# Another order of steps on four engines, in all four phases of a hybrid block kernel

## The reference

```
def first_block(x, meta_tokens, ...):
    h = jnp.concatenate([meta, x], axis=1)                # 272 tokens
    p = rms_norm(h, norm_mix_pre[l]) @ w_in[l]
    oa = rg_lru_group(xa, ya, ...)                        # causal conv, gates, associative scan, gelu
    ob = forgetting_attention_group(q, k, v, f_logit, ..) # 8 heads of 64
    oc, v_own = rwkv7_group(pc, ...)                      # 4 heads of 64, state S per step
    mixed = jnp.concatenate([oa, ob, oc], axis=-1) @ w_out[l]
    h = h + rms_norm(mixed, norm_mix_post[l])
    f = causal_dwconv(rms_norm(h, norm_ffn_pre[l]) @ ffn_up[l], ffn_conv[l])   # 1024 -> 5632
    gate, val = jnp.split(f, 2, axis=-1)
    h = h + rms_norm((gelu(gate) * val) @ ffn_down[l], norm_ffn_post[l])
    return h[:, N_META:]

def second_block(x, ...):
    for l in range(2):
        proj = rmsnorm(x, pre_g[l]) @ w_in[l]
        y_a = sgu_mixer(...) * silu(z_a)                  # layernorm, 128x128 mixing per group
        y_b = mla_mixer(...) * silu(z_b)                  # low-rank attention with rope
        y_c = chunk_band_mixer(...) * silu(z_c)           # banded attention with relative bias
        br = einsum(ys, w_branch[l]);  gates = sigmoid(g_logits + gate_b[l])
        x = x + rmsnorm(sum(gates * br) @ w_out[l], post_g[l])
```

## Time and profile before

| | us |
|---|---|
| median of 3 runs | 941.23 |
| lowest, highest | 940.35, 943.87 |
| span of the profiled execution | 940.6 |
| PE busy | 918.4 (98%) |
| PE weight loads busy | 855.0 (91%) |
| DVE busy | 696.6 (74%) |
| ACT busy | 521.6 (55%) |
| POOL busy | 226.8 (24%) |
| DMA | 150.32 MB, mean 160 GB/s |

### The profile page before, as it was taken

The page is one execution under the profiler, slowest core; times in us unless marked ns, Lnnn a source line. Parts: engine busy times, 40 slices in busy tenths (PEclk is TensorE's granted clock), DMA queues, the critical chain, the costliest instruction groups (busy, mean ns, idle before and its releaser), DMA issues.

```text
span 940.6 us, 19615 instructions
## 1 busy us (share of the span) xinstructions
PE 918.4 (98%) x7924; PEld 855.0 (91%) x7924; DVE 696.6 (74%) x1072; ACT 521.6 (55%) x942; POOL 226.8 (24%) x194
## 2 busy tenths in 40 slices
...
GB/s 320 180 157 113 70 26 2 68 113 180 183 189 185 184 178 180 170 176 245 179 140 153 152 136 203 192 188 181 100 305 152 146 125 177 183 178 181 159 201 45
DMA packets 41705, 150.32 MB, mean 160 GB/s; under 512 B 4624, under 2 KB 5008, under 8 KB 41360
## 3 DMA queue, kind: packets, MB, share of 16 engines
...
## 4 chain that ended last, share of the span: by engine, by line
PE 89%; DVE 4%; ACT 2%; issue 2%; DMA 1%; POOL 1%; DVEq 0%; SPq 0%; ACTq 0%; POOLq 0%
PE ps L736 87%; PE ps L1073 2%; DVE wlo L1713 1%; DMA raw<-in_ws 1%; DVE S L1713 1%; ACT whi L1297 1%; PE ps L1189 0%; DMA h<-in_hT 0%; ACT xh L1297 0%; DVE xl L1721 0%; POOL ocf L2306 0%; ACT L1297 0%; ACT tmp L1297 0%; DVE ht L1721 0%; DVE pcraw L1713 0%
## 5 line engine op out<-in xcount | busy, mean ns | idle before, releaser
L1297 ACT ACTIVATE whi<-raw 128x1024 fp32r<-128x1024 f32 (+1 forms) x265 | 278.2, 1052 | 282.1 <-PE ps L736 276.5
L736 PE MATMUL ps<-xh,whi 128*128 128x256 f32 (+2 forms) x1440 | 412.9, 287 | 4.5 <-ACT xh L1297 1.8
L736 PE MATMUL ps<-xl,whi 128*128 128x256 f32 (+2 forms) x1440 | 407.9, 283 | 2.3 <-DVE xl L1721 2.2
L736 PE MATMUL ps<-xh,wlo 128*128 128x256 f32 (+2 forms) x1440 | 407.0, 283 | 0.0
L1713 DVE TENSOR_TENSOR wlo<-raw,whi 128x1024 fp32r<-128x1024 f32 (+1 forms) x257 | 328.0, 1281 | 103.8 <-ACT whi L1297 103.1
L736 PEld LDWEIGHTS ps<-xh,whi 128*128 128x128 f32 x1440 | 271.5, 189 | 10.9 <-issue 8.3
L736 PEld LDWEIGHTS ps<-xl,whi 128*128 128x128 f32 x1440 | 270.9, 188 | 3.9 <-DVE xl L1721 3.5
L736 PEld LDWEIGHTS ps<-xh,wlo 128*128 128x128 f32 x1440 | 272.0, 189 | 0.0
L736 PE MATMUL ps<-yh,whi 128*128 128x256 f32 x232 | 65.3, 282 | 0.0
L736 PE MATMUL ps<-yl,whi 128*128 128x256 f32 x232 | 65.2, 281 | 0.0
L736 PE MATMUL ps<-yh,wlo 128*128 128x256 f32 x232 | 65.2, 281 | 0.0
...
## 6 DMA issues: line engine op xcount, KB each, us to landing
raw<-in_ws SPq DMA_DIRECT2D x261, 512.0 KB, 3.4
...
```

The costliest lines, as they stand in the source:

```text
L736: return e.matmul(o, l, r, start=start, stop=stop, skip_group_check=True)
L1297: return e.activation(o, a, f, bias=bias, scale=scale, accum_out=acc)
```

## The change

Only the letter strings of `WEAVE` change, those of PE, DVE, ACT and POOL in each of the four phases; SP's strings stay. In each phase every letter stands as often as before in an engine's string, so each engine does the same steps and the same instructions, and within a line in the same order; what changes is how the lines are woven. The semaphore waits follow from the events as before.

- Start: on ACT `la.a` moves from ahead of `inend` to behind split 16; parts of entering tiles stand ahead of splits, and on POOL the first square sums.
- Mixer: on PE the dense tiles of A stand ahead of later doubling steps; `beat` 0 to 4 leave the scan and the output steps and stand in a row ahead of the first `op`, `beat` 5 and 6 stand behind `opend`. On DVE, splits 25 and 26 move from around `lr.tan` 0 to behind attention tile 5; `lr.b` and the LRU scan go to a later place. On ACT, `rw.o` 1 goes ahead of a copy of attention tile 4.
- First seam: on DVE split 35 moves from behind residual 0 to behind all eight entering tiles, on ACT as well.
- Feed-forward and layers: on DVE, ACT and POOL, splits stand in runs of three to six instead of by turns with the evacuations; POOL takes no weight part from unit 35 on, so its "w" letters there issue nothing.

The diff, cut to the mixer, and DVE's string of the feed-forward (the others and the layers' are changed in the same manner):

```diff
 WEAVE = {
     "mixer": {
         "pe": (
-            "ddddddddddfdddddddddrddddddrrdddddddrrrddddfdddddddrrddeddrrrsssdrdrdlrdrdldrddrssrseeessseosoorre"
-            "eerrrrrrozrororeroozrerereeozozrorrroeozerrzorzrroppppppppp"
+            "ddddddddddfddddddrddddddddrrddddrrrfddddddddrrddddddddrrreddddsssdeddddrlrrlerreddrsssrsssoersrero"
+            "orrrrrorroreoooreerereerooroorrreererroorrozzzzzpppppppppzz"
+        ),
+        "dve": (
+            "dwdwdmdwdddwdsdddddwwmmwdwmfmddmwwwdrdrwdmdrfwwwrrrrrdrddwwwmfrdddwwrrwmrrdssrrrewddwwssnssddelder"
+            "rlrwewdrrllrsessslssoorrdorererrrrrreoorrrooerlooollrreeereoowwosreerrroorrccccpppwwwwwpppwwpwpp"
         ),
         "act": (
-            "eodwdwdddwwddwdsdndwwwwfwwrwsrwwrwrrrrwrrwwwrrwwdddddwwrrwwserewlrwlwlrdwdresslseesocorrrererooooo"
-            "eeceoooeeroerroerrrrroocccpwwpwppwpwpwpwpp"
-        ),
-        "dve": (
-            "dmwdwdddwwwdddsdnddwddfwwwdmdfdwwmwsrrddmdmmdwwrdwmmwwmddwdrrwrrrrdwwdrsssdfwrrrwerwrrrwddssrdreee"
-            "edlrwdlrrwldwwldrrssssslssoolllrroererrrerrororooreroooerrcerereooreoeroorrrrcccpwwpwwpppwpwpwpp"
+            "dwedwddwddwdddwsdwwwwrrrwwworfwwwrrrrrrwwwnswwrrrddddwwwwwwsdeerlrllrdersswwweesoosrldrrerooooeeee"
+            "ooooeecrrcoreorrrrerroocccppwwppwwwwpppwpp"
         ),
         "pool": (
-            "wwewwedmoopdddddddwdwwwmmwwwwmmwwwwrrmrmmwwwwrrrwwwwsswrrrwwreeeweerrwwwwllcoooooeeeeeoooooceeeooo"
-            "rrcpppwwwwpppp"
+            "dwwdddmdddddwwowwwmmwwmrewwrwwmmmwmrwwwwrrrwwwwwwwseerrrrrsrwoooeeeeeeooopooowwwolwwleeeeeeooooccr"
+            "recpppwppwpwwp"
         ),
...
     "ffn": {
...
+        "dve": (
+            "hhhdhhdddhhhddddwwwddddcdwwwwccwddcvvcdddccvdwwwwdccwddwwvccvcwddwwcccddvcwdddvwwwwvcccdddcdwwwvvc"
+            "ccwwwddvcccvddwwwddvcccdddwwwwwvccccddddvvwwwcccdddwwvvwwwwwwccwwcdddvwwwwwcccdccwwwwwvvvwwww000w0"
+            "00w101101110w000011111110w1ww"
         ),
...
-        "dve": (
-            "hwdhhhhdhddhhddwddwwdddwddwcdwcdwvcwdcdwvcwdcwdvcdwcwdvcwdcwdvwcdwcdwvcdwcwdvcwdcwdvcwdcwdvwcdwcdw"
-            "vcwdcwdvcwdcdvwcwdcwvdcwdcwdvwcdwcdwvcwdcdwvcdwcvwdcdwcdvwcwdcvwdcdwcwdvcwcvwccvwwwwwwwwwwwww0000w"
-            "0011w0101110w1101000011111www"
-        ),
```

More of the change, by code:

```diff
@@ L264 @@
         "pe": (
[L265 to L266 removed]
+            "ddddddddddfddddddrddddddddrrddddrrrfddddddddrrddddddddrrreddddsssdeddddrlrrlerreddrsssrsssoersrero"
[4 more added lines that the diff above has]
+            "rlrwewdrrllrsessslssoorrdorererrrrrreoorrrooerlooollrreeereoowwosreerrroorrccccpppwwwwwpppwwpwpp"
         ),
         "act": (
[L269 to L274 removed]
+            "dwedwddwddwdddwsdwwwwrrrwwworfwwwrrrrrrwwwnswwrrrddddwwwwwwsdeerlrllrdersswwweesoosrldrrerooooeeee"
+            "ooooeecrrcoreorrrrerroocccppwwppwwwwpppwpp"
         ),
         "pool": (
[L277 to L278 removed]
+            "dwwdddmdddddwwowwwwmmwwmrewwrwwmmmwmrwwwwrrrwwwwwwwseerrrrrsrwoooeeeeeooopooowwwolwwleeeeeeooooccr"
+            "recpppwppwpwwp"
         ),
@@ L285 @@
         "pe": (
-            "ddqdddddddddddddddddddddddddddddddddddddddddddddqdddqqdppppppppppppppppppppppppppppppppppppppppppp"
-            "p00pp1100p11pppppr"
+            "ddqddddddddddddqdddddddddddddddddqddddddddddddddddqddddppppppppppppppppppppppppppppppppppppppppppp"
+            "p00pp1001ppp11pppr"
+        ),
+        "dve": (
+            "hhhdhhdddhhhddddwwwddddcdwwwwccwddcvvcdddccvdwwwwdccwddwwvccvcwddwwcccddvcwdddvwwwwvcccdddcdwwwvvc"
+            "ccwwwddvcccvddwwwddvcccdddwwwwwvccccddddvvwwwcccdddwwvvwwwwwwccwwcdddvwwwwwcccdccwwwwwvvvwwww000w0"
+            "00w101101110w000011111110w1ww"
         ),
         "act": (
-            "wddddqddwddwbwdwccwccwvwccwvvwccwvvwcwvvccwwvcvwcwvcwvcwcwvvwcwvvcwcwvcvwcwvcwvcwcwvvwcwvvcwccvwvw"
-            "cwvcvwcwcvwvcwcwvvwqccwvvwcvwqvqccwcvwvwcvwcvcwwvcvwvwvwvbwwwwwwwwwww00w00w01w00111111000001111w1w"
+            "ddddddddwwwwdccccwwwwvvvcccvvwwwcvvbccwcwwwwvvvcwvwwccccvvqcwqwwwwvvcccvvccwwvvvcwwwcwqvvvcccwwvvv"
+            "cccwwwwwvvvccccwvvvvccwwwqccwwwvvwwccwvwwwvvwwwwwwvccccwwwwvvvvvwwwwb000w0w01w001111100001110w111w"
             "wrrr"
         ),
-        "dve": (
-            "hwdhhhhdhddhhddwddwwdddwddwcdwcdwvcwdcdwvcwdcwdvcdwcwdvcwdcwdvwcdwcdwvcdwcwdvcwdcwdvcwdcwdvwcdwcdw"
-            "vcwdcwdvcwdcdvwcwdcwvdcwdcwdvwcdwcdwvcwdcdwvcdwcvwdcdwcdvwcwdcvwdcdwcwdvcwcvwccvwwwwwwwwwwwww0000w"
-            "0011w0101110w1101000011111www"
-        ),
         "pool": (
-            "dwwwwwwwwwwwwhwwwwwwwwwwwwwwwwwwwwwwwwwwwwwwwwwwwwwwwwwwwwwwwwwwwwwwwwwwhhhhhhhdddddddvvvvvvvvvvvv"
-            "vvvvvvvvvv"
+            "hwwwwwwwwwwhwwwwddwwwwwwwwhhwwhhddddddwwwwvwwwwwvwvvvwwwwwwwwwwwvvwwwwvvvwwwvvwwhwwwwwvvvvvwvvwwww"
+            "wwwhvvvwww"
         ),
@@ L308 @@
         "pe": (
-            "dddddtdtdddddeoododddddddddeeeddeoddoddeooeeoddedeedodooeoeedeeeeddddddddddddoodooeoodedddodossddd"
-            "dddddddddddddddddddddddddddddddddddddddddpppppppppppppppp00p11p0011ppprppp"
+            "dddddtdtdddddeoddddddddddeedddddedeooodoooeeeddddedeeoodedooooeeddeeddddeeddddoeoooedddddooddddsso"
+            "dddddddddddddddddddddddddddddddddddddddddpppppppppppppppp00p11p0011ppppppr"
+        ),
+        "dve": (
+            "wwddddwwdwdwttddwwwwdddeeeddwwwddddddowwooddwwwwwyyoeeoeeddddeyyoowddwwwoeeeeeewwoddddoooyyyyyywww"
+            "eeeuuyywwwweoouuwwooossssssosswwweeddddwwwwoodddwwddwwwddddwwwddsswwwdddddwwwwwdddwwddddddwdddwwdd"
+            "ddwwwdddddwwwmddmmmmdddddwwwwmmmwwww000w0001w111011001110w00001111w1ww"
         ),
         "act": (
[L313 to L320, removed]
+            "wwwwawwtttwowwwwweeeddwdddddwwddwooewwddwwoeeeddwwwwooodeeeewweoeooeddddddswwwweooodeewwwwwoeessso"
+            "oosssswwwwddddowowwwwwwoewwwwsswwwwwdddddddddddddddwwwwwwwwbmdddwwddmmmwwwwmmwwwmmwwwwwb00w000w111"
+            "001111w000001111w1wrrrw"
         ),
         "pool": (
-            "oeoeyyyyyyyywwwwwwwwwwwwwwwwwwwwwwwwwwwwwwwwwwwwwwwwwwwwwwwwwwwwwwwwwwwwwwwwwwwwwwwwwwwwwwwwwwwsss"
-            "saaaateedoodeooeoeeeoeeeeeooooooyeeeeeyyyoooooesssssossmmmmmmmm"
+            "wwwwwwwysssayatwwwywawwwwwawwwswwwwwwweeeooowdweeeewwwyyydeywwwwwowwwwwwwwwoooooeeyyywwwwwwwwwwwww"
+            "wwwwwwwwywwwwwwooowweeeywwwwwwwwwooooooeeeeeessssseoossmmmmmmmm"
         ),
```

20 lines of the change are left out of this document (9 added, 11 removed).

## The result

The changed kernel takes 951.5 us (median of 4 runs, 949.75 to 952.21) against 941.24 for the one before: ratio 1.0102, 95% interval 1.0087 to 1.0117. Forecast were 933 and a range of 928 to 943. The profiled execution's span is 950.3 us, 9.7 over the 940.6 of before. No instruction was added. PE's busy time rose from 918.4 to 925.1, DVE's fell from 696.6 to 687.7, and POOL's from 226.8 to 213.0 us.

A forecast was written before the change was run, and what follows sets the result against it. PE, busy 98% of the span, was taken as the bound. Terms for start, mixer, seams, up-projection and layers summed to 8.3 us gained from 940.6, giving 932.3; 0.6 to the median made 932.9, forecast 933, range 928 to 943.

The forecast's parts named there:

- The bound: Whole kernel: PE busy 98% of the span; gains only where PE waits, runs at half clock or does filler.
- The seam: Seam 1: `xl` up to 1.75 us earlier, plus 0.75 from less half clock behind it; 2.5 forecast.
- the middle: Mixer, 110–142: two PE waits go, 1.9 us, and beat 0 leaves, 0.7; sum 2.6.
- the up-projection: Feed-forward: batches of splits make PE wait once, -1.0 us; ends 0 and -14.
- seams 2 and 3: Splits move from ahead of the awaited `xl`; half of 2.5 us of waits goes, gain 1.2.
- The scan term: Mixer, 142–154: beats 1 to 3 leave the scan; half of their 1.69 us gained, 0.8.
- The start: Before the first shift: `la.a` and splits out of the way shorten three PE waits; gain 1.4 us.
- The layers' term: Two layers: two evacuations late by half a split, 0.6 us each; -1.2, ends 0 and -5.
- A: Mixer scan and tail: latency and two half-clock stretches take the gain back; 938.7 us, chance 0.18.
- Rival B: Up-projection: batches of splits starve PE at each of some twelve batches; 946.8 us, chance 0.12.
- the ring's lead: Up-projection: four split buffers give 11.6 us of PE work against 8.9 needed, so the lead holds by 2.7.
- The tail: Mixer, 155.6-176: earlier copy of `o`, earlier variance, beats out and less slow clock; gain 2.0 us.

The follow-up runs named there:

- combined kernel: Changed kernel with the layers' strings of before, POOL's split 27 behind its LRU products and DVE's `init2` behind the last entering tile: 937.2 us, ratio 0.9956; repeated, 936.9.

## Why the prediction was wrong

Two steps failed: the scan was costed as if only its beats moved (+0.8, measured -5.9), and the layers as two evacuations late by 0.6 each (-1.2, measured -9.6). In their place the runs showed a DVE instruction held by POOL with PE's next step queued behind it, and a clock that fell more.

**The bound** held: the change could gain only where PE waits or is slow, and those places were the right ones for the gains. The seam, the middle, the up-projection and seams 2 and 3 came within 0.1 to 0.7 us of their terms (2.2 of 2.5, 2.7 of 2.6, -0.9 of -1.0, 1.9 of 1.2). Part of that is luck. In the middle both old waits went, but a new one of 0.87 us for `rw_X` came at 104.16, against the sign "no PE wait over 0.5 us": PE's idle time fell by 0.9 and not 1.9, the beat gave 0.7, and the other 1.1 is time in which PE counts as busy.

```profile
104.16 1.50 PE L736 MATMUL ps<-rw_X,rw_x 64*64 64x64 f32 x40 [0.87 <-DVE rw_X L1713]
```

At seam 1 PE idles 2.2 us less and the clock gave 1.8, more than the two terms, and beats 5 and 6, which the prediction set at nothing, take 1.2 of it. `xl` is waited for 0.74 us instead of 1.55, and the clock in 205–210 was 1.00:

```profile
205.78 0.48 DVE L1721 SCALAR_TENSOR_TENSOR xl<-h,col,xh 128x258 fp32r<-128x258 f32 x1
...
206.31 0.38 PE L736 MATMUL ps<-xl,whi 128*128 128x258 f32 x1 [0.74 <-DVE xl L1721]
```

**The scan term**, +0.8 for -5.9: I costed the beats and nothing else there. The change also moved `lr.b` and the LRU scans into the scan, between `rw.scanS` 2 and `rw.scanU` 3. I had written them off as a gain where they left ("the same holds with `rw.levb` 4"), not as a cost where they went. And POOL's split 27 met them there; with it moved, 4.7 of the 5.9 us came back. Even the beats had the wrong sign: moved out by themselves they cost 6 to 7 us. The move of a step has two ends, and I priced one.

**The start** failed in the same manner: `la.a` out of the way let the root wait for PE alone (ACT's wait of 4.60 us before 20.65), but POOL's split moved beside `init2`, and PE waited 0.93 us for the last `xl`. The first shifted tile came at 23.63, where 21.6 was forecast. With `init2` behind that `xl` in the combined kernel, the start's stretch was 1.2 us ahead of before instead of 0.6 behind. Of the 1.8 us between the two, 1.2 fall at this `xl`. The rest lies ahead of it, where matmuls ran slowly for longer in this execution, which the windows' clock doesn't show (1.00). The same matmul before and after:

```profile
7.06 0.29 PE L736 MATMUL ps<-xh,wlo 128*128 128x272 f32 x1
```

```profile
7.21 0.43 PE L736 MATMUL ps<-xh,wlo 128*128 128x272 f32 x1
```

**The layers' term** was mis-sized, -1.2 for -9.6. "Each time a tile's evacuation is late by half a split" took a split at 1.24 us. Beside POOL it is 2.3, a run of three is 5.7, and there were not two such places but many, of which the larger three cost 0.6 to 2.0 each. One of them wasn't a batch at all, but a copy behind a waiting Tanh on ACT. The size of the rest, some 6 us, stays unexplained.

**The clock** had a rival of its own (A, 0.18, 938.7), and its sign came: a clock under 1.0 in more than two 5-us windows. It priced 6.0 us more at half clock; the trace has 10.0 more in 140–165. I put it beside the beats only. The runs show it beside PE's waits as well (removing the wait of 2.33 us raised the clock in that stretch from 0.77 to 0.86), but don't show what decides it.

**Rival B** had the sign right and the place wrong. The up-projection, with DVE at 89% of the window, lost 0.9 us; the layers, with DVE at 73%, lost nine. Why the ring's lead covers batches there and not in the layers is argued, not shown: POOL is busy 15% of the up-projection's window (17.73 of 117) and 23% of the layers', and the attention chain of the layers needs one particular small step.

**The tail** gave 0.5 for 2.0, within it the low clock at 160–165.
